# The first mixer of the second block in even and odd tokens, its Fourier half and long convolution as one stage; gates projected in strips, softmax weights blended on queries

## The chip, the cores and the metric

One core of a Trainium2 chip runs the whole program in one launch. TensorE multiplies, VectorE, ScalarE and GpSimd work elementwise, SyncE issues the DMAs. The metric is the device time of one execution in microseconds (us), lower is better. Before the change it is 3509.33 us, the median of 3 runs (3504.07 to 3513.66).

## The reference, cut to what matters

Two blocks of two layers each, 512 tokens, width 1024, all in float32. The change touches four places. Only they are shown.

```python
# first block, layer 0: the gates of the delta rule, from 32 columns of the projection
g = -jnp.exp(a_log) * jax.nn.softplus(a + dt_bias); beta = jax.nn.sigmoid(b)
q = l2norm(q) * DK ** -0.5; k = l2norm(k)
# first block, layer 1: three head groups of window attention, weighed against each other
alpha = jax.nn.softmax(jnp.stack(lses, axis=2), axis=2)
o = (o * alpha[..., None]).reshape(B, S, DSWA_WIDTH)
# second block, layer 0: the mixer, for x (L = 512) and for the context (L = 256)
u_f = proj[..., :512].reshape(B, L, 4, 128)
y_f = jnp.fft.fft2(u_f, axes=(1, 3), norm='ortho').real.reshape(B, L, 512)
x0, x1, v = jnp.split(_dwconv3(proj[..., 512:], conv_w, conv_b), 3, axis=-1)
spectrum = _hyena_filter_spectrum(L, ...)   # h @ w4, times a decay, two-sided, divided by sum |.|, rfft
y_h = x0 * (irfft(rfft(v * x1, n=2 * L) * spectrum)[:, :L] + v * x1 * bias)
return jnp.concatenate([y_f, y_h], axis=-1) @ w_out
```

## The kernel before

Activations lie with features on the 128 partitions and tokens along the free dimension. The program is a row of stages (`Core.stage`). Within a stage each engine has its own instruction list, written by hand, and the engines wait for each other on semaphores. Between stages all engines meet at a barrier (L155 to L157), so a stage ends with its slowest engine and nothing of the next stage begins earlier. Only weights run ahead: SyncE (`stream_weights`) keeps a ring of 4 chunks of 512 KB filled past the stage's end. A large weight product splits both operands into a high and a low part in fp32r and adds three products (L264 to L266). The small transforms are plain F32 products, and each of them leaves two records in the trace.

The stages that the change touches:

- **gdn_gates** (L751). TensorE projects 512 tokens onto 32 gate columns (L778: 4 token chunks times 8 k-tiles, tokens stationary, 32 columns moving). VectorE copies the result (L812) and computes the gates from it, with ScalarE between. GpSimd squares the keys (L803) and ScalarE the queries. TensorE sums the squares in four 32-column strips of the array (L786), VectorE takes reciprocals (L836), TensorE spreads them (L798) and VectorE scales (L846).
- **blend** (L1917). Maxima and sums, queries on partitions, are transposed to 6 rows of heads by 3 x 512 (L1940, L1958). VectorE and ScalarE work the softmax out on 6 partitions (L1961 to L1970). TensorE spreads it over the 9 tiles (L1948), VectorE multiplies (L1974).
- **filter** (L2092). For each of 6 token blocks and 2 directions TensorE makes the taps (L2137), VectorE applies the decay (L2171), ScalarE takes absolute values (L2197), TensorE sums them over partitions with a matrix of ones (L2130). Then come the transforms of the taps (L2151), 40 products of 512 columns, which VectorE scales into `Hr`, `Hi` (L2183). The final norm of the first block rides along on VectorE (L394, L340, L407, L409).
- **mixer_in** (L2223), the input product, is not touched.
- **fourier** (L2286). For each of 4 channel groups TensorE makes 6 half sums (L2310), VectorE copies them (L2331), TensorE mixes tokens (L2320: 8 products of 512 columns for x, 4 of 256 for the context), ScalarE copies out (L2338).
- **hyena** (L2341). VectorE gates (L2404), TensorE transposes to tokens (L2367), transforms (L2379: 32 and 8 products of 512 columns), VectorE multiplies spectra (L2409 to L2412), TensorE transforms back (L2390: 32 of 512 columns, 16 of 256), VectorE adds and gates (L2421, L2424). The tables are loaded by SyncE at the start of each stage (L2213).

## Time and profile before

| | |
|---|---|
| median of 3 runs | 3509.33 us |
| profiled execution | 3512.14 us |
| its span, first to last instruction | 3510.1 us |
| TensorE busy | 3232.0 us (92%) |
| VectorE busy | 1640.7 us (47%) |
| GpSimd busy | 1089.9 us (31%) |
| ScalarE busy | 1019.8 us (29%) |
| mean granted TensorE clock | 0.95 |

The clock is a share of 2.4 GHz; 0.50 is 1.2 GHz, and a stretch in between holds both levels. Busy time of TensorE counts a pipelined product until its end, so neighbours overlap: products are priced here by the distance of their starts. Lines are those of the kernel before. In the trace `ctx` stands for the filter's sines too, which share its memory.

### The profile page before, as it was taken

The numbers are of one execution on the slowest core, as the hardware profiler recorded it, in microseconds if no ns is written. First come the engines' busy times: TensorE is split into PE (matmuls) and PEld (weight loads), VectorE is DVE, ScalarE is ACT, GpSimd is POOL, SyncE is SP. The second block draws the span as 40 slices with busy tenths as digits, with TensorE's granted clock in tenths as the row PEclk, the third lists the DMA queues.
The fourth block names the chain that finished last, engine by engine and source line by source line (L and its number), as shares of the span: only waits on it lengthen the run. The fifth ranks groups of instructions, "written<-read, shape, count | busy, mean of one in ns | idle before, by whom it ended". The sixth has DMA issues, their size and how long they took to land. (4 is left out here: it accounts for less than half of the span.)

```text
span 3510.1 us, 55525 instructions
## 1 busy us (share of the span) xinstructions
PE 3232.0 (92%) x21706; PEld 2523.5 (72%) x21706; DVE 1640.7 (47%) x2413; ACT 1019.8 (29%) x1532; POOL 1089.9 (31%) x518
## 2 busy tenths in 40 slices
PE   7987888999999789999898799999999889899999
PEld 6855666787878567878386368888888433389987
DVE  6834543421131635311675346555555556557741
ACT  4322332212221622122120013222224324343322
POOL 3422112454444024444021012222222015534433
PEclk9978989999999989999899999999999979999999
DMA  3225334222223012222211111111121111122222
GB/s 133 93 91 172 112 126 154 90 96 90 96 88 118 1 63 94 91 91 100 88 60 61 60 36 60 60 66 60 54 66 54 42 46 44 29 79 90 94 85 84
DMA packets 79885, 282.19 MB, mean 80 GB/s; under 512 B 9386, under 2 KB 12272, under 8 KB 78845
## 3 DMA queue, kind: packets, MB, share of 16 engines
q1 hardware_dynamic: 79164, 279.52, 24.2%
q8 instruction: 106, 1.74, 0.2%
q10 hardware_dynamic: 576, 0.62, 0.1%
q14 instruction: 39, 0.31, 0.0%
HBM read 270.12 MB, written 2.12 MB: 78 GB/s over the span
## 5 line engine op out<-in xcount | busy, mean ns | idle before, releaser
L207 POOL TENSOR_TENSOR weights_low<-weight_ring,weights_high 128x1024 fp32r<-128x1024 f32 x359 | 890.7, 2481 | 1825.4 <-ACT weights_high L201 1825.4
L201 ACT ACTIVATE weights_high<-weight_ring 128x1024 fp32r<-128x1024 f32 x372 | 392.2, 1054 | 852.6 <-PE bank L266 842.3
L264 PE MATMUL bank<-ffn_in_high,weights_low 128*128 128x258 f32 (+2 forms) x1408 | 438.3, 311 | 10.6 <-DVE ffn_in_low L470 6.5
L266 PE MATMUL bank<-ffn_in_high,weights_high 128*128 128x258 f32 (+2 forms) x1408 | 437.8, 311 | 0.0
L265 PE MATMUL bank<-ffn_in_low,weights_high 128*128 128x258 f32 (+2 forms) x1408 | 437.4, 311 | 0.0
L264 PEld LDWEIGHTS bank<-ffn_in_high,weights_low 128*128 128x128 f32 x1408 | 266.7, 189 | 26.8 <-issue 7.1
L265 PEld LDWEIGHTS bank<-ffn_in_low,weights_high 128*128 128x128 f32 x1408 | 267.3, 190 | 14.7
L266 PEld LDWEIGHTS bank<-ffn_in_high,weights_high 128*128 128x128 f32 x1408 | 266.1, 189 | 14.2
L264 PE MATMUL bank<-mlp_down_high,weights_low 128*128 128x512 f32 x512 | 200.5, 392 | 8.0 <-DVE mlp_down_low L570 8.0
L264 PE MATMUL bank<-mlp_in_high,weights_low 128*128 128x512 f32 x512 | 201.8, 394 | 6.2 <-DVE mlp_in_low L470 6.2
L264 PE MATMUL bank<-ffn_down_high,weights_low 128*128 128x512 f32 (+1 forms) x528 | 189.6, 359 | 11.9 <-DVE ffn_down_low L570 11.9
L265 PE MATMUL bank<-mlp_in_low,weights_high 128*128 128x512 f32 x512 | 200.5, 392 | 0.0
L266 PE MATMUL bank<-mlp_in_high,weights_high 128*128 128x512 f32 x512 | 200.5, 392 | 0.0
L265 PE MATMUL bank<-mlp_down_low,weights_high 128*128 128x512 f32 x512 | 200.4, 391 | 0.0
L266 PE MATMUL bank<-mlp_down_high,weights_high 128*128 128x512 f32 x512 | 200.3, 391 | 0.0
L570 DVE TENSOR_TENSOR ffn_down_low<-ffn_hidden,ffn_down_high 128x1024 fp32r<-128x1024 f32 (+1 forms) x66 | 101.6, 1569 | 190.4 <-ACT ffn_down_high L527 190.4
L265 PE MATMUL bank<-ffn_down_low,weights_high 128*128 128x512 f32 (+1 forms) x528 | 189.6, 359 | 0.0
L266 PE MATMUL bank<-ffn_down_high,weights_high 128*128 128x512 f32 (+1 forms) x528 | 188.4, 357 | 0.0
L570 DVE TENSOR_TENSOR mlp_down_low<-mlp_hidden,mlp_down_high 128x512 fp32r<-128x512 f32 x64 | 44.2, 693 | 293.4 <-ACT mlp_down_high L527 293.4
L638 DVE SCALAR_TENSOR_TENSOR mlp_relu<-bank,rstd 128x512 f32<-128x512 f32 x64 | 44.2, 690 | 195.9 <-PE bank L266 195.7
L264 PE MATMUL bank<-gdn_in_high,weights_low 128*128 128x512 f32 x256 | 102.4, 400 | 20.0 <-DVE gdn_in_low L470 20.0
L264 PEld LDWEIGHTS bank<-ffn_down_high,weights_low 128*128 128x128 f32 x528 | 101.2, 192 | 27.3 <-issue 12.3
(541 smaller groups left out, 6463.9 us busy)
## 6 DMA issues: line engine op xcount, KB each, us to landing
weight_ring<-in_mod SPq DMA_DIRECT2D x96, 512.0 KB, 4.4
weight_ring<-in_ffn_up SPq DMA_DIRECT2D x88, 512.0 KB, 3.5
weight_ring<-in_mlp_up SPq DMA_DIRECT2D x64, 512.0 KB, 3.5
weight_ring<-in_mlp_down SPq DMA_DIRECT2D x64, 512.0 KB, 3.5
weight_ring<-in_ffn_down SPq DMA_DIRECT2D x44, 512.0 KB, 3.5
weight_ring<-in_gdn_in SPq DMA_DIRECT2D x32, 512.0 KB, 3.5
weight_ring<-in_dswa_in SPq DMA_DIRECT2D x27, 512.0 KB, 3.5
weight_ring<-in_fh_in SPq DMA_DIRECT2D x16, 512.0 KB, 3.5
```

The costliest lines, as they stand in the source:

```text
L201: act.activation(self.high[:, (g.s0 + at) % SPLIT, 0:g.floats], raw, ACT.Copy).then_inc(self.high_ready, 1)
L207: pool.tensor_tensor(self.low[:, slot, 0:g.floats], self.ring[:, (g.c0 + at) % RING, 0:g.floats], self.high[:, slot, 0:g.floats], ALU.subt ...
L264: pe.matmul(bank, wl, ah, start=start, stop=False)
L265: pe.matmul(bank, wh, al, start=False, stop=False)
L266: return pe.matmul(bank, wh, ah, start=False, stop=stop)
L570: last = dve.tensor_tensor(low[:, at % 2, :, lo:lo + tokens], src((n - p * PER_PASS) * KC, KC), high[:, at % 2, :, lo:lo + tokens], ALU.su ...
L638: dve.scalar_tensor_tensor(out=relu[:, at % 2, :], in0=core.ps[at % RING][:, :], scalar=0.0, in1=core.rstd[:, 0, :], op0=ALU.max, op1=ALU. ...
```

## The change

In the mixer all tables over tokens are laid out with the even tokens first and then the odd ones, and only half of the frequencies are computed as products. The sums over the even and over the odd tokens are kept apart. One frequency of the lower half is odd sum plus even sum, its mirror is the difference. This holds for the filter's taps, for the gated input, for the way back, and for the tokens of the Fourier half. `fourier` and `hyena` become one stage, `mixer_middle`, whose TensorE list interleaves them. The inverse tables are loaded into the memory of the forward ones once the forward transforms are done. Divisions by the filter's absolute sums move from the spectra to the results (`inv_sum`), and the sums are made with the taps stationary and two columns of ones moving. In the gates eight products with 32 stationary columns run in four strips of the array, and four products with stacked identities add the strips. In the blend the softmax is done with queries on partitions, and the weights are turned once, split in fp32r, and spread from 18 rows.

```diff
     @block.tensor
     def _(pe):
+        for k in range(KD):
+            m = pe.matmul(strip(core.ps[0], k % 4)[:, :], wab[:, k, :], core.h[:, k, :], start=k < 4, stop=k >= KD - 4)
+        m.then_inc(strip_sums, 1)
+        pe.wait_ge(strips_kept, 1)
         for c in range(NCH):
-            for k in range(KD):
-                m = pe.matmul(ps_ab[:, c, :], core.h[:, k, c * CH:(c + 1) * CH], wab[:, k, :],
-                              start=k == 0, stop=k == KD - 1)
+            m = pe.matmul(ps_ab[:, c, :], by_strip[:, c * CH:(c + 1) * CH], eye, start=True, stop=True)
         m.then_inc(projected, 1)
...
+        dve.wait_ge(strip_sums, 1)
+        dve.tensor_copy(by_strip[:, :], core.ps[0][:, :]).then_inc(strips_kept, 1)
         dve.wait_ge(projected, 1)
         o(dve.tensor_copy(ab[:, :, :], ps_ab))
...
+    @block.gpsimd
+    def _(pool):
+        pool.wait_ge(loaded, 16)
+        pool.tensor_copy(sel[:, :, :], rows[:, :, :]).then_inc(sel_ready, 1)
...
+        act.wait_ge(turned, 1)
+        act.activation(by_residue(high[:, :]), TURNED[0:3 * HG, :].rearrange("h (r m) -> h r m", r=4), ACT.Copy).then_inc(alpha_high, 1)
...
+        near = stats[:, :, 0, :].rearrange("p x (h b) -> p b x h", b=4)
+        for r in range(4):
+            for b in range(4):
+                last = pe.matmul(NEAR[32 * b:32 * b + 32, 2 * HG * r:2 * HG * (r + 1)], core.ident[:, r::4], near[:, b, :, :],
+                                 start=True, stop=True)
+        last.then_inc(reordered, 1)
+        pe.wait_ge(weighed, 1)
+        alphas = maxes.rearrange("p g (h r) -> p r (g h)", r=4)
+        for r in range(4):
+            last = pe.transpose(TURNED[0:3 * HG, r * P:(r + 1) * P], alphas[:, r, :], core.ident[:, :])
+        last.then_inc(turned, 1)
+        pe.wait_ge(sel_ready, 1)
+        pe.wait_ge(alpha_high, 1)
         for n in range(DW_TILES):
             if n >= 4:
                 pe.wait_ge(blended, n - 3)
-            pe.matmul(core.ps[n % 4][:, :], sel[:, n % GT, :], rows[:, n // GT, :], start=True, stop=True).then_inc(spread, 1)
...
+        dve.wait_ge(reordered, 1)
+        o(dve.tensor_copy(stats[:, :, 0, :].rearrange("p x (h r) -> p x h r", r=4),
+                          NEAR[:, 0:8 * HG].rearrange("p (r x h) -> p x h r", r=4, x=2)))
+        o(dve.tensor_reduce(top[:, :], by_group(maxes), AX, ALU.min))
+        dve.tensor_tensor(maxes, over(top), maxes, ALU.subtract).then_inc(centred, 1)
         dve.wait_ge(exped, 1)
...
+        o(dve.tensor_tensor(sums, sums, maxes, ALU.mult))
+        o(dve.tensor_reduce(total[:, :], by_group(sums), AX, ALU.add))
+        o(dve.reciprocal(total[:, :], total[:, :]))
+        dve.tensor_tensor(maxes, maxes, over(total), ALU.mult).then_inc(weighed, 1)
+        dve.wait_ge(alpha_high, 1)
+        dve.tensor_tensor(by_residue(low[:, :]), TURNED[0:3 * HG, :].rearrange("h (r m) -> h r m", r=4), by_residue(high[:, :]),
+                          ALU.subtract).then_inc(alpha_low, 1)
...
+BANDS = [(s, ft) for s, (lo, L, b0, nb) in enumerate(STREAMS) for ft in range(nb // 2)]
+PARITY_BLOCKS = [(s, q, j) for s, (lo, L, b0, nb) in enumerate(STREAMS) for q in range(2) for j in range(nb // 2)]
+def parity_block(n, lo=0):
+    s, q, j = PARITY_BLOCKS[n]
+    return slice(lo + 2 * P * j + q, lo + 2 * P * (j + 1), 2)
+def half_spectrum(pe, banks, table, part, pair, tokens_of):
+    s, ft = BANDS[pair]
+    lo, L, b0, nb = STREAMS[s]
+    for q in range(2):
+for j in range(nb // 2):
+    b = q * nb // 2 + j
+    last = pe.matmul(banks[q][:, :], table.forward(part, s, b, ft), tokens_of(b0 + b), start=j == 0, stop=j == nb // 2 - 1)
+    return last
+def both_halves(dve, part, lower, mirrored, even, odd):
+    first = dve.tensor_tensor(lower, odd, even, ALU.add)
+    if part == 0:
+return first, dve.tensor_tensor(mirrored, even, odd, ALU.subtract)
+    return first, dve.tensor_tensor(mirrored, odd, even, ALU.subtract)
...
-                pe.matmul(ps[4 + s][:, :], core.ones[:, :], ab[:, d, :], start=b == b0 and d == 0,
-                          stop=b == b0 + nb - 1 and d == 1).then_inc(normed, 1)
+                for c in range(G):
+                    col = 2 * (G * s + c)
+                    last = pe.matmul(ps[4][:, col:col + 2], ab[:, d, c * P:(c + 1) * P], core.ones[:, 0:2], start=b + d + c == 0,
+                                     stop=b == BLOCKS - 1 and d == 1 and c == G - 1)
+                last.then_inc(summed, 1)
...
+        for p, (s, ft) in enumerate(BANDS):
+            lo, L, b0, nb = STREAMS[s]
             pe.wait_ge(mixed, b0 + nb)
...
+            for part in range(2):
+                g = 2 * p + part
+                if g == 2:
+                    norm.tensor(pe)
+                    pe.wait_ge(mixed, BLOCKS)
+                if g >= 3:
+                    pe.wait_ge(taken, g - 2)
+                half_spectrum(pe, GROUP(g), dft, part, p, lambda n: f[:, part, n, :]).then_inc(spectra, 1)
...
+        for g in range(2 * len(BANDS)):
+            p, part = g // 2, g % 2
+            H = (Hr, Hi)[part]
+            dve.wait_ge(odd_ready, g + 1)
+            first, second = both_halves(dve, part, H[:, p, 0, :], H[:, p, 1, :], GROUP(g)[0][:, :], odd[:, g % 3, :])
+            second.then_inc(taken, 1)
+            if g == 2:
+                norm.scale(dve, norm_order)
+        dve.wait_ge(summed, 2 * BLOCKS)
+        dve.reciprocal(inv_sum[:, :], ps[4][:, 0:4 * G])
...
+        for g in range(2 * len(BANDS)):
+            act.wait_ge(spectra, g + 1)
+            if g >= 3:
+                act.wait_ge(taken, g - 2)
+            act.activation(odd[:, g % 3, :], GROUP(g)[1][:, :], ACT.Copy).then_inc(odd_ready, 1)
+            if g == 2:
+                norm.roots(act)
...
-def fourier_stage(core, a, tables):
+def mixer_middle_stage(core, a, uh, Hr, Hi, inv_sum, dft, inverse, fourier):
...
+GROUP = lambda g: ((ps[2], ps[3]), (ps[4], ps[5]), (ps[0], ps[1]), (ps[6], ps[7]), (ps[0], ps[1]), (ps[6], ps[7]))[g]
+HALF = lambda m: ps[2 + m % 2][:, 0:2 * P]
+FOURIER = lambda s: ps[4 + s][:, 0:STREAMS[s][1]]
+CONVOLVED = lambda n: ps[2 + n % 2][:, 0:STREAMS[n // G][1]]
...
+        dft.load(sp, dft_loaded)
+        sp.dma_start(chan[:, :], a["fourier_channels"]).then_inc(channels_loaded, 16)
+        fourier.load(sp, fourier_loaded)
+        sp.wait_ge(spectra, 2 * len(BANDS))
+        inverse.load(sp, inverse_loaded)
...
+        def turn(i):
+            n = TURNS[i]
+            s = PARITY_BLOCKS[n][0]
+            pe.wait_ge(gated, i // 2 + 1)
+            if i >= 2:
+                pe.wait_ge(ptok_ready, i - 1)
+            for c in range(G):
+                last = pe.transpose(ps[i % 2][:, c * P:(c + 1) * P], uh[:, 2 * G + c, parity_block(n, START[s])], core.ident[:, :])
+            last.then_inc(turned, 1)
...
+        def halves(gr):
+            for n in range(BLOCKS):
+                m = gr * BLOCKS + n
+                if m >= 2:
+                    pe.wait_ge(halved, m - 1)
+                pe.matmul(HALF(m), tokens(gr, n), chan[:, :], start=True, stop=True).then_inc(half_sums, 1)
+        def mix(gr):
+            pe.wait_ge(halved, (gr + 1) * BLOCKS)
+            for s, (lo, L, b0, nb) in enumerate(STREAMS):
+                if gr:
+                    pe.wait_ge(fourier_kept, 2 * (gr - 1) + s + 1)
+                for q in range(2):
+                    for j in range(nb // 2):
+                        b = q * nb // 2 + j
                         for part in range(2):
...
+                            last = pe.matmul(FOURIER(s)[:, q * L // 2:(q + 1) * L // 2], af[:, gr % 2, b0 + b, part * P:(part + 1) * P],
+                                             fourier.rows(part, s, b), start=j == 0 and part == 0, stop=j == nb // 2 - 1 and part == 1)
+                last.then_inc(fourier_ready, 1)
+        def convolved(n):
+            s, c = n // G, n % G
+            lo, L, b0, nb = STREAMS[s]
+            if n >= 2:
+                pe.wait_ge(y_scaled, n - 1)
+            for q in range(2):
+                for kb in range(nb // 2):
+                    for part, H in enumerate((Hr, Hi)):
+                        last = pe.matmul(CONVOLVED(n)[:, q * L // 2:(q + 1) * L // 2], H[:, b0 // 2 + kb, q, c * P:(c + 1) * P],
+                                         inverse.rows(part, s, kb)[:, q * L // 2:(q + 1) * L // 2],
+                                         start=kb == 0 and part == 0, stop=kb == nb // 2 - 1 and part == 1)
+            last.then_inc(y_sums, 1)
...
+        for i in range(BLOCKS):
+            turn(i)
+        pe.wait_ge(ptok_ready, BLOCKS)
+        pe.wait_ge(dft_loaded, 16 * dft.loads)
+        spectrum(0)
+        spectrum(1)
+        pe.wait_ge(channels_loaded, 16)
+        pe.wait_ge(taken, 1)
+        halves(0)
+        halves(1)
+        pe.wait_ge(fourier_loaded, 16 * fourier.loads)
+        pe.wait_ge(taken, 2)
+        mix(0)
+        spectrum(2)
+        halves(2)
+        mix(1)
+        halves(3)
+        mix(2)
+        mix(3)
+        pe.wait_ge(inverse_loaded, 16 * inverse.loads)
+        pe.wait_ge(products, 2)
+        for n in range(G):
+            convolved(n)
+        pe.wait_ge(products, 3)
+        for n in range(G, 2 * G):
...
+        def odd_sums(g):
+            act.wait_ge(spectra, g + 1)
+            if g >= 2:
+                act.wait_ge(taken, g - 1)
+            act.activation(odd[:, g % 2, :], GROUP(g)[1][:, :], ACT.Copy).then_inc(odd_ready, 1)
...
+        for lo, hi in ((0, T // 2), (T // 2, T), (CTX0, CTX0 + TC)):
+            v = uh[:, 2 * G:3 * G, lo:hi]
+            dve.tensor_tensor(v, v, uh[:, G:2 * G, lo:hi], ALU.mult).then_inc(gated, 1)
+        for p in range(len(BANDS)):
+            if p:
+                dve.wait_ge(products, p)
+            for part in range(2):
+                g = 2 * p + part
+                dve.wait_ge(odd_ready, g + 1)
+                first, second = both_halves(dve, part, X[:, part, 0, :], X[:, part, 1, :], GROUP(g)[0][:, :], odd[:, g % 2, :])
+                second.then_inc(taken, 1)
+            hr, hi = Hr[:, p, :, :], Hi[:, p, :, :]
+            Xr, Xi = X[:, 0, :, :], X[:, 1, :, :]
+            dve.wait_ge(taken, 2 * p + 2)
+            o.add(dve.tensor_tensor(Y[:, :, :], Xr, hr, ALU.mult))
+            o(dve.tensor_tensor(Xr, Xr, hi, ALU.mult))
+            o.add(dve.tensor_tensor(hi, Xi, hi, ALU.mult))
+            o(dve.tensor_tensor(hr, Xi, hr, ALU.mult))
+            o.add(dve.tensor_tensor(Y[:, :, :], Y[:, :, :], hi, ALU.add))
+            o(dve.tensor_tensor(Xr, hr, Xr, ALU.subtract))
+            dve.tensor_tensor(Hr[:, p, 0, :], Y[:, 0, :], Y[:, 1, :], ALU.add)
+            dve.tensor_tensor(Hr[:, p, 1, :], Y[:, 0, :], Y[:, 1, :], ALU.subtract)
+            dve.tensor_tensor(Hi[:, p, 0, :], X[:, 0, 0, :], X[:, 0, 1, :], ALU.subtract)
+            dve.tensor_tensor(Hi[:, p, 1, :], X[:, 0, 0, :], X[:, 0, 1, :], ALU.add).then_inc(products, 1)
...
+parity = np.concatenate([np.arange(0, L, 2), np.arange(1, L, 2)])
+odd, whole_ = odd[parity, :L // 2], whole_[parity, :L // 2]
```

TensorE in the filter stage, before: the last taps (`filt_w`), the absolute sums (`filt_abs`), the transforms (`filt_taps`) and the norm's sum (L349).

```order
L2137 MATMUL bank<-filt_w,ctx 128x512 x2
L2130 MATMUL bank<-filt_abs,ones 128x512 x2
L2137 MATMUL bank<-filt_w,ctx 128x512 x2
L2130 MATMUL bank<-filt_abs,ones 128x512 x4
L2151 MATMUL bank<-filt_taps,filter_dft_x 128x512 x16
L349 MATMUL bank<-mix_h,ones 128x512
L2151 MATMUL bank<-filt_taps,filter_dft_x 128x512 x16
L2151 MATMUL bank<-filt_taps,filter_dft_ctx 128x512 x8
```

The same place now:

```order
L2219 MATMUL bank<-filt_w,ctx 128x512 x2
L2211 MATMUL bank<-ones,filt_abs 128x2 x8
L2219 MATMUL bank<-filt_w,ctx 128x512 x2
L2211 MATMUL bank<-ones,filt_abs 128x2 x16
L2159 MATMUL bank<-filt_taps,filter_dft_x 128x512 x8
L349 MATMUL bank<-mix_h,ones 128x512
L2159 MATMUL bank<-filt_taps,filter_dft_x 128x512 x8
L2159 MATMUL bank<-filt_taps,filter_dft_ctx 128x512 x4
```

The 12 absolute sums of 512 columns are 48 of two columns, and the 40 transforms are 20.

VectorE at the end of the filter stage, now, behind the norm's sums (`rstd`, `x` are the norm's scaling; `filt_odd_sums` the odd sums that ScalarE copied). Before, the products of L407 and L409 had ten scalings of `Hr` and `Hi` around them and a reciprocal of 512 columns (L2179) ahead of each stream.

```order
L2165 TENSOR_TENSOR Hr<-filt_odd_sums,bank 128x512
L2167 TENSOR_TENSOR Hr<-bank,filt_odd_sums 128x512
L407 RECIPROCAL rstd<-rstd 128x512
L409 SCALAR_TENSOR_TENSOR x<-x,params,rstd 128x512 x8
L2165 TENSOR_TENSOR Hi<-filt_odd_sums,bank 128x512
L2168 TENSOR_TENSOR Hi<-filt_odd_sums,bank 128x512
L2165 TENSOR_TENSOR Hr<-filt_odd_sums,bank 128x512
L2167 TENSOR_TENSOR Hr<-bank,filt_odd_sums 128x512
L2165 TENSOR_TENSOR Hi<-filt_odd_sums,bank 128x512
L2168 TENSOR_TENSOR Hi<-filt_odd_sums,bank 128x512
L2264 RECIPROCAL hyena_inv_sum<-bank 128x16
```

Six sums and differences stand behind the norm's scaling.

TensorE between mixer_in and mixer_out, before, from the end of the Fourier stage into the long convolution:

```order
L2320 MATMUL bank<-fourier_dft_x,fourier_half 128x512 x8
L2320 MATMUL bank<-fourier_dft_ctx,fourier_half 128x256 x4
L155 UNCONDITIONAL_BRANCH
L2358 UNCONDITIONAL_BRANCH
L2367 MATMUL bank<-ident,hyena_in 128x128 x24
L2379 MATMUL bank<-gated_tok,dft_x 128x512 x32
L2379 MATMUL bank<-gated_tok,dft_ctx 128x512 x8
```

Now, the beginning of the one stage (`hyena_in` behind L2418 is the memory of the Fourier half sums):

```order
L2392 MATMUL bank<-ident,hyena_in 128x128 x24
L2159 MATMUL bank<-mid_gated_tok,dft_x 128x512 x16
L2407 MATMUL bank<-mid_channels,mix_h 128x256 x4
L2407 MATMUL bank<-mid_channels,mix_h_ctx 128x256 x2
L2407 MATMUL bank<-mid_channels,mix_h 128x256 x4
L2407 MATMUL bank<-mid_channels,mix_h_ctx 128x256 x2
L2418 MATMUL bank<-fourier_dft_x,hyena_in 128x256 x8
L2418 MATMUL bank<-fourier_dft_ctx,hyena_in 128x128 x4
L2159 MATMUL bank<-mid_gated_tok,dft_ctx 128x512 x4
```

The barrier is gone, the transposes and 16 transforms come first, the Fourier half stands between them and the way back, and each mix has half the columns.

## Rows read from the trace of the kernel before

**Rows 1.** By stretches: length; busy of PE, PEld, DVE, ACT, POOL; PEclk; DMA share; GB/s.
```profile
204.90:240.70 35.80, 29.89 (x134) 20.71 (x134) 18.87 (x40) 11.07 (x16) 7.44 (x4) 0.61 0.00 0
1214.40:1251.20 36.80, 20.97 (x42) 8.79 (x42) 22.60 (x23) 1.48 (x1) 0.00 (x0) 0.55 0.00 0
1674.70:1710.50 35.80, 32.15 (x48) 11.08 (x49) 15.66 (x24) 10.42 (x14) 0.00 (x0) 0.68 0.53 193
1710.50:1749.40 38.90, 35.42 (x83) 15.31 (x81) 29.70 (x28) 1.02 (x3) 0.00 (x0) 1.00 0.01 5
...
1898.00:1956.80 58.80, 47.50 (x144) 29.07 (x144) 10.19 (x24) 3.92 (x8) 0.00 (x0) 0.87 0.12 47
1956.80:2053.30 96.50, 78.41 (x200) 38.40 (x200) 35.93 (x53) 3.48 (x6) 0.00 (x0) 0.91 0.14 55
```

**Rows 2.** Timeline, gates stage: start us, us, engine line op out<-in xcount [idle before].
```profile
204.91 12.57 PE L778 MATMUL bank<-w_ab,gdn_h 128*128 128x32 f32 x64 [2.15 <-PEq L157]
217.41 4.88 PE L786 MATMUL bank<-gdn_squares,one_column 128*32 128x512 f32 x32
...
204.89 7.45 POOL L803 TENSOR_TENSOR gdn_squares<-conv 128x1024 f32<-128x1024 f32 x4 [9.77 <-SPq L155]
```

**Rows 3.** Timeline, TensorE: spread of the blend and products of the next stage.
```profile
1234.10 15.70 PE L1948 MATMUL bank<-blend_maxima,head_rows 6*128 6x512 f32 x18 [14.36 <-DVE blend_maxima L1970]
...
1253.43 0.63 PE L265 MATMUL bank<-window_out_low,weights_high 128*128 128x512 f32 x1
1253.85 0.63 PE L266 MATMUL bank<-window_out_high,weights_high 128*128 128x512 f32 x1
```

**Rows 4.** Timeline, filter stage: TensorE, then VectorE, then ScalarE.
```profile
1678.35 7.19 PE L2137 MATMUL bank<-filt_w,ctx 64*128 64x512 f32 x8 [6.82 <-DMA filt_w<-in_filter_w]
...
1702.98 1.98 PE L2130 MATMUL bank<-filt_abs,ones 128*128 128x512 f32 x4
...
1710.53 13.90 PE L2151 MATMUL bank<-filt_taps,filter_dft_x 128*128 128x512 f32 x32
...
1732.80 3.34 DVE L407 RECIPROCAL rstd<-rstd 128x512 f32<-128x512 f32 x1
1736.18 5.39 DVE L409 SCALAR_TENSOR_TENSOR x<-x,params,rstd 128x512 f32<-128x512 f32 x8
...
1709.53 1.28 ACT L353 ACT_TABLE_LOAD   x1
```

**Rows 5.** By stretches, columns as in rows 1, inside the gates and filter stages.
```profile
208.00:211.00 3.00, 3.00 (x16) 3.00 (x15) 0.00 (x0) 2.17 (x3) 3.00 (x3) 0.50 0.00 0
...
1682.00:1690.00 8.00, 8.00 (x10) 2.55 (x9) 3.37 (x5) 1.89 (x3) 0.00 (x0) 0.50 1.06 426
```

**Rows 6.** Timeline, Fourier stage: TensorE, then ScalarE.
```profile
1907.87 3.78 PE L2310 MATMUL bank<-fourier_channels,mix_h 128*128 128x256 f32 x8 [15.91 <-DMA fourier_dft_ctx<-in_fourier_ctx]
...
1915.66 7.03 PE L2320 MATMUL bank<-fourier_dft_x,fourier_half 128*128 128x512 f32 x16
1922.52 1.89 PE L2320 MATMUL bank<-fourier_dft_ctx,fourier_half 128*128 128x256 f32 x8
...
1922.72 0.60 ACT L2338 ACTIVATE mix_h<-bank 128x512 f32<-128x512 f32 x1 [38.15 <-PE bank L2320]
```

**Rows 7.** Timeline, long convolution: TensorE, then VectorE.
```profile
1960.24 4.66 PE L2367 MATMUL bank<-ident,hyena_in 128*128 128x128 f32 x24 [4.87 <-DVE hyena_in L2404]
1972.63 30.28 PE L2379 MATMUL bank<-gated_tok,dft_x 128*128 128x512 f32 x64 [7.73 <-DMA inverse_dft_ctx<-in_inverse_ctx]
...
1956.82 3.37 DVE L2404 TENSOR_TENSOR hyena_in<-hyena_in 128x3080 f32<-128x3080 f32 x1 [18.17 <-PEq L157]
```

**Rows 8.** Timeline, last tiles of the mixer's input product: VectorE, then GpSimd.
```profile
1884.76 2.85 DVE L2277 TENSOR_SCALAR hy_padded<-hy_padded,mixer_shift 128x512 f32<-128x512 f32 x2 [0.16 <-DVE hy_padded L485]
...
1893.24 0.75 DVE L2277 TENSOR_SCALAR hy_padded<-hy_padded,mixer_shift 128x512 f32<-128x512 f32 x2 [0.16 <-DVE hy_padded L485]
...
1884.65 2.40 POOL L214 TENSOR_TENSOR weights_low<-weight_ring,weights_high 128x1024 fp32r<-128x1024 f32 x1 [6.09 <-ACT weights_high L201]
```

More of the change, by code:

```diff
@@ L2089, in scalar, with __init__, tiles, load @@
         act.activation(self.sn[:, :], self.u[:, :], ACT.Sin).then_inc(self.sines, 1)
-def hyena_filter_stage(core, a, sn, Hr, Hi, cs, norm, loads):
+class Tables:
+    loads = 2
+    def __init__(self, a, key, tiles, inverse=False):
+        blocks = lambda L: L // P // 2 if inverse else L // P
+        self.tabs = [t[:, :].rearrange("p (c b n) -> p c b n", c=2, b=blocks(L)) for t, L in zip(tiles, (T, TC))]
+        self.src = a[key + "_x"], a[key + "_ctx"]
+    @staticmethod
+    def tiles(core, ctx, name):
+        return core.sb(name + "_x", [P, T // P * T], ctx), core.sb(name + "_ctx", [P, TC // P * TC], ctx)
+    def load(self, eng, sem):
+        for dst, src in zip(self.tabs, self.src):
+            eng.dma_start(dst, src).then_inc(sem, 16)
+    def rows(self, part, s, b):
+        return self.tabs[s][:, part, b, :]
+    def forward(self, part, s, b, ft):
+        return self.rows(part, s, b)[:, ft * P:(ft + 1) * P]
+BANDS = [(s, ft) for s, (lo, L, b0, nb) in enumerate(STREAMS) for ft in range(nb // 2)]
[16 more added lines that the diff above has]
+    return first, dve.tensor_tensor(mirrored, odd, even, ALU.subtract)
+def hyena_filter_stage(core, a, sn, Hr, Hi, inv_sum, dft, norm, loads):
     with ExitStack() as ctx:
@@ L3308, in program @@
[L3308 to L3309 removed]
+                with ExitStack() as inner:
+                    parts = [core.halves("mix_in", T, inner), core.halves("mix_in_ctx", TC + 2, inner)]
+                    norm = LateNorm(core, [(x, core.h, T, mod[0].gain(0, 0), parts[0]), (xc, core.hc, TC, mod[0].gain(0, 1), parts[1])],
+                                    [mod[0].shift(0, s) for s in range(2)])
+                    mixer_in_stage(core, gemm["fh_in"], norm, parts, uh)
```

336 lines of the change are left out of this document (121 added, 215 removed).

## The prediction

> **What bounds the kernel now.** I read the page's engine table first: TensorE is busy 92% of the span and no other engine half of it, so what leaves TensorE's list counts in full, if the stage stays TensorE's. The query by stretches then gives each touched stage its length, because a barrier closes every stage and a saving in one can't be eaten by another [rows 1]: gates 35.8 us, blend 36.8, filter 35.8 + 38.9, Fourier 58.8, long convolution 96.5. Third came the timelines of these stages, for the prices of products and for who ends last [rows 2 to 4, 6, 7]. Fourth, the clock inside stretches [rows 5]. The reader is to see three kinds of stage: the two of the mixer are TensorE's with holes for DMA and handshakes, the blend is a chain of small steps on 6 partitions, and the filter is half at 1.2 GHz.
>
> Prices: an F32 product of 512 columns takes two records of (1922.52 - 1915.66) / 16 = 0.43 us, so 0.86, at 2.4 GHz, and half of it for 256 columns [rows 6]. At 1.2 GHz it is twice that (15.70 / 9 = 1.74 [rows 3]). An fp32r product at 1.2 GHz starts 0.42 behind its neighbour [rows 3]. VectorE takes 5.39 / 8 = 0.67 per 512 [rows 4] and 3.37 x 1024 / 3080 = 1.12 per 1024 [rows 7], ScalarE 0.60 [rows 6]. A hop between engines I take as 0.2 (TensorE's last product of L2320 for x ends at 1922.7, the copy begins at 1922.72 [rows 6], other hops are longer).
>
> **Middle stage, before 58.8 + 96.5 = 155.3 us.** TensorE's list now: 24 transposes at 4.66 / 24 [rows 7] = 5.2 with ScalarE's copies; 20 transforms x 0.86 = 17.2, with some 2.6 for the low level at their start, as 32 of them took 30.28 for 27.5 [rows 7]; 24 half sums; 4 mixes of 8 x 0.43 + 4 x 0.25 = 4.4, so 17.6; 16 x 2 products of 256 columns and 16 of 128 on the way back, 13.7 + 4.1 = 17.8. The half sums have two banks where they had four and ScalarE in VectorE's place: two products of 0.43, each waiting for the copy two before it (0.38 and two hops), give 0.55 each, 13.2.
> The start: VectorE's first gate is a third of 3.37, TensorE begins at 1.4 and its transforms at 7.4. The tables for them are half of what the Fourier stage loaded, which were there 10 us after that stage began (first product at 1907.87 [rows 6], stage from 1898.0 [rows 1]); with some 2 us of latency in both I expect them at 6, hidden. End of TensorE: 7.4 + 17.2 + 2.6 + 13.2 + 17.6 + 17.8 + 0.6 of hops = 76.4. Then ScalarE, VectorE twice on 256 columns and the barrier, 2.6: **79**. Nothing else is late: VectorE needs 4 x 0.65 + 6 x 1.15 + 4 x 0.65 = 12.1 per band, three bands from 14 to 53, and the first way back at about 58.5 wants two of them. The inverse tables are asked for behind the last transform at 38.5, with 20 us to land. Saving 76.3. Bounds: if the half sums go at 0.43 and the low level costs nothing, 73.5; if every half sum takes a full round of 1.0 and the mixes lose 2 each on waits, 98.
>
> **Filter, before 35.8 + 38.9.** Taps: 12 products unchanged. The sums of absolutes: 48 products x 2 records, each with a 128-column load and two moving columns. The nearest row is L778, which moves 32 columns: 12.57 / 64 = 0.196 per record [rows 2], so 18.9. Before, 12 products of 0.96 (1.98 less the tail, for two) at 2.4 GHz or 1.86 at 1.2 [rows 4]. By level alone this is a draw: the change here is what the level does. While TensorE issued L778 back to back the granted clock was 0.50 [rows 5], and in this stage it stayed at 0.50 from 1682 to 1690 though TensorE was busy all 8.00 us. In that stretch half of the work has only 64 rows; the level rose once blocks with all 128 rows had run, and in the new list there is no such block before the transforms. So I take 1.2 GHz for all of it: taps 12 x 1.78 (7.19 for four [rows 4]) = 21.4, sums 19 to 20.4, handoffs 1, 42 instead of 32.2 from 1678.35 on: +9.8. The Trainium skill, "TensorE: Matmul & The Clock Gate", Part 1, says that sustained TensorE activity brings the full clock; by it the level would rise soon after the stage's start, which is rival B.
> Second half: 8 transforms at the low level's start 9.5, the norm's sum 0.86, 4 more, 13.8. VectorE is then ahead. But the root now stands behind three copies on ScalarE: copy 14.6, its table load 1.28 [rows 4], root, 16.6; reciprocal 3.34 and scaling 5.39 [rows 4] to 25.4; three pairs of sum and difference, 3.8; end and barrier 30.4, VectorE's, against 38.9: -8.5. Filter **+1.3**. Bounds: -13 (level rises as before) to +6 (records of the sums at 0.25, pairs at 2.0).
>
> **Gates, before 35.8.** L778's 12.57 becomes: 8 products in strips, two rounds of four; L786 did four rounds in 4.88 [rows 2], so 2.4; hop, VectorE copy 0.7, hop; 8 records of 0.2, 1.6: 5.1. That is 7.5 earlier, and the VectorE chain behind it moves whole. One cover goes: GpSimd's squares end at 204.89 + 7.45 = 212.3 [rows 2], before the old chain began, but beside the new one (from 210). VectorE beside GpSimd waits: the same two instructions took 2.85 beside a GpSimd piece and 0.75 alone [rows 8]. So 0 to 2.3, I take 1.2. The Trainium skill, "SBUF — State Buffer", section "SBUF: two separate sides", has it as a lock held for the whole GpSimd instruction, which would let VectorE in after the current piece, near the 1.2. Gates **-6.3** (-5.2 to -8.3).
>
> **Blend, before 36.8.** 16 products of 12 columns with 32-column loads: between 1.6 (a quarter of L778's record) and 6.2 (its whole), I take 2.5, as strips overlap [rows 2]. VectorE's seven short steps and ScalarE's exponential on 128 partitions, 72 or 24 wide, 2.9 with hops, in place of four of 1.7 and a reciprocal on 6 partitions; turning 1.0, ScalarE's copy 0.8. The spread: 18 fp32r products x 0.42 = 7.7 instead of 15.70 (1.2 GHz in both [rows 1, 3]); the low half is made beside the first high product, 0.6 shows. Last VectorE step and barrier 1.3; GpSimd casts the selection beside VectorE's steps, 0 to 2.4, taken 1.2: 18. Gain **-18.8** (-15 to -20).
>
> **Sum.** -76.3 + 1.3 - 6.3 - 18.8 = -100.1. The profiled execution took 3512.14 (span 3510.1, 2.0 around it), so 3412.0. It stood 2.8 over the median; half of that off: 3411.
>
> **The rivals.** A is this forecast, its own range 3401 to 3424.
> B: the filter's first half reaches 2.4 GHz as before. For: the old list did, in the middle of it. Against: two-column products move hardly anything, and L778 lost the level with sixteen times as many. First half unchanged instead of +9.8, second part starts at full clock and ends 27 instead of 30.4: 13.2 less, **3398**.
> C: the middle stage becomes a chain of handshakes: half sums at 1.0, a mix waiting for its two copies, way back waiting for VectorE's products. For: ScalarE serves four kinds of bank in a fixed order. Against: every copy is shorter than the products beside it. +15, **3426**.
> D, slower: the low level outlives the stages. If the two-column sums and the short 128-column products put TensorE to 1.2 GHz and it doesn't come back in the GEMMs behind, each us of them costs one more. It decides at about 100 us of such work, i.e. mixer_out and a quarter of the feed-forward product behind it; carried through 150 us the time is 3411 + 150 = **3561**. For: the level fell under a busy TensorE once. Against: the Fourier stage is at full clock within 5 us (0.87 over 58.8 with 10 idle [rows 1]).
> That the sums are not halved is excluded by the order: 20 transforms, halves of columns in all mixes.
>
> **How the numbers follow.** A 0.60, B 0.20, C 0.17, D 0.01, the rest below 3388. The likeliest is 3411. The range goes from 3390, with B and its spread, to 3432, with C. What can be told from no change is 0.3%, 10.5 us. Only D and what lies near it is above 3520: slower 0.01, same 0.01, faster 0.98.
>
> **What would show it.** In the stretches: middle stage 75 to 84 us with TensorE's clock near 0.95 and VectorE under 60% busy; if it is over 90, the waits in front of L2407 or L2418 name C. Filter: the stretch of taps and sums at 0.50 throughout and about 42 us (A) or 32 with 1.00 in its second half (B), then VectorE as the last engine for 10 us with TensorE idle. Gates: L778 in two rounds of 1.2, VectorE steps stretched before 212. Blend: fp32r pairs 0.85 apart. I am wrong in the main point if the middle stage isn't TensorE's, or if products with 8-byte steps between tokens take longer than 0.43 per record of 512 columns, which no row before shows.

## The result, and the profile after

The changed kernel takes **3408.24 us** (median of 4 runs, 3406.26 to 3411.66) against 3509.18 us of the kernel before on the same chip: a ratio of **0.9714**, 95% interval 0.9697 to 0.9731. The forecast was 3411, its range 3390 to 3432. The profiled execution has a span of 3406.2 us at a mean clock of 0.951, against 3510.1 at 0.950: nothing came from the clock as a whole.

The stages by stretches, in the columns of [rows 1]: gates, blend, filter up to its first transform, filter from there, middle stage.

```profile
203.85:234.15 30.30, 23.63 (x94) 10.96 (x94) 20.95 (x41) 11.07 (x16) 7.44 (x5) 0.57 0.00 1
...
1209.15:1225.00 15.85, 10.09 (x54) 6.67 (x54) 9.39 (x17) 1.32 (x2) 1.13 (x1) 0.50 0.02 5
...
1649.40:1695.80 46.40, 42.71 (x120) 27.73 (x120) 17.15 (x25) 9.46 (x13) 0.00 (x0) 0.50 0.35 125
1695.80:1725.20 29.40, 20.27 (x44) 8.75 (x43) 21.76 (x26) 5.55 (x8) 0.00 (x0) 0.85 0.00 0
...
1873.10:1950.40 77.30, 71.14 (x304) 51.87 (x304) 52.58 (x65) 25.47 (x60) 0.00 (x0) 0.95 0.14 53
```

Set against [rows 1], term by term:

| part | before | after | forecast | measured |
|---|---|---|---|---|
| gates | 35.8 | 30.3 | -6.3 | -5.5 |
| blend | 36.8 | 15.85 | -18.8 | -20.95 |
| filter, taps and sums | 35.8 | 46.4 | +9.8 | +10.6 |
| filter, transforms | 38.9 | 29.4 | -8.5 | -9.5 |
| middle stage | 155.3 | 76.65 | -76.3 | -78.65 |
| sum of the four stages | | | -100.1 | -104.0 |

For the middle stage the stretch above begins 0.65 us too early: the first instruction of the stage, the load of a table, starts at 1873.76. From there to the next stage it is 76.65, and these are the marks of [rows 1]; the texts of the runs below still say 77.3. The untouched stages are 0.1 longer (span -103.9). The medians differ by 100.9, since the profiled execution of before stood 2.8 over its median.

TensorE in the middle stage, by start and length, with the pieces in front and the way back left out:

```profile
1875.09 5.72 PE L2392 MATMUL bank<-ident,hyena_in 128*128 128x128 f32 x24 [7.43 <-DVE hyena_in L2513]
...
1881.49 14.00 PE L2159 MATMUL bank<-mid_gated_tok,dft_x 128*128 128x512 f32 x32 [0.69 <-ACT mid_gated_tok L2486]
1895.33 2.26 PE L2407 MATMUL bank<-mid_channels,mix_h 128*128 128x256 f32 x8
...
1902.16 3.62 PE L2418 MATMUL bank<-fourier_dft_x,hyena_in 128*128 128x256 f32 x16
...
1906.50 3.60 PE L2159 MATMUL bank<-mid_gated_tok,dft_ctx 128*128 128x512 f32 x8
1909.93 2.26 PE L2407 MATMUL bank<-mid_channels,mix_h 128*128 128x256 f32 x8
...
1929.67 0.60 PE L2430 MATMUL bank<-dft_x,Hr 128*128 128x256 f32 x2
```

Between the transforms and the way back TensorE has no wait but the handshakes within the half sums, and the other products keep their prices: 16 transforms in 13.84 and 4 in 3.43, a mix in 4.34, the way back in 17.7. TensorE is idle for 5.5 us of 76.65, where the two stages before held 29.4 of idle time in 155.3.

The end of the filter stage, VectorE:

```profile
1711.87 3.35 DVE L407 RECIPROCAL rstd<-rstd 128x512 f32<-128x512 f32 x1 [0.71 <-ACT rstd L353]
1715.26 5.39 DVE L409 SCALAR_TENSOR_TENSOR x<-x,params,rstd 128x512 f32<-128x512 f32 x8
1720.57 0.68 DVE L2165 TENSOR_TENSOR Hi<-filt_odd_sums,bank 128x512 f32<-128x512 f32 x1
...
1724.15 0.26 DVE L2264 RECIPROCAL hyena_inv_sum<-bank 128x16 f32<-128x16 f32 x1
```

TensorE's last four transforms begin at 1712.47 and take 3.60: it is done 8 us before VectorE.

### The profile page after: what moved, and what is told of

Read it like the earlier page. It is cut to its first block and busy times, and to the rows that moved or that the text cites. A ratio compares the mean times of both kernels' runs of the same rounds, so it can differ in the third digit from the quotient of the medians.

```text
span 3406.2 us, 55466 instructions
## 1 busy us (share of the span) xinstructions
PE 3156.1 (93%) x21670; PEld 2507.6 (74%) x21670; DVE 1629.8 (48%) x2395; ACT 1041.5 (31%) x1585; POOL 1089.0 (32%) x519
## 3 DMA queue, kind: packets, MB, share of 16 engines
q1 hardware_dynamic: 79179, 274.35, 24.6%
## 5 line engine op out<-in xcount | busy, mean ns | idle before, releaser
L264 PE MATMUL bank<-ffn_in_high,weights_low 128*128 128x258 f32 (+2 forms) x1408 | 438.4, 311 | 10.6 <-DVE ffn_in_low L470 6.6
L2622 DVE TENSOR_SCALAR ffn_padded<-ffn_padded,ffn_shift 128x512 f32<-128x512 f32 (+1 forms) x88 | 117.4, 1376 | 6.8 <-DVE ffn_padded L485 6.5
```

The source lines that it names most:

```text
L264: pe.matmul(bank, wl, ah, start=start, stop=False)
L2622: o.add(dve.tensor_scalar(dst, dst, shift[:, j % 2, 0, s:s + 1], None, ALU.add))
```

## The experiments

Twelve kernels ran. Each is the changed kernel with the edit shown. A stage length is from the profiled execution, a ratio is against the kernel before on the same chip, with its interval; the changed kernel's is 0.9714 (0.9697 to 0.9731). A ratio tells some 6 us at best: where its interval overlaps the changed kernel's, as with the norm in front, the pairs, the third band and the squares, the reading rests on the stage in the trace alone.

**1. The filter's first stretch: is it the sums, the rows, or neither?** Four kernels; the first stretch goes from the load of the taps' weights to the first transform, the rest from there to the next stage. In the changed kernel and in the five of the twelve that leave this stage alone the taps and sums ran at the prices of 0.50 to the end, so the level there is no accident of one execution.

Absolute sums with 512 moving columns:

```diff
-for c in range(G):
-    pe.matmul(ps[4][:, col:col + 2], ab[:, d, c * P:(c + 1) * P], core.ones[:, 0:2], ...)
+pe.matmul(ps[4 + 2 * s][:, :], core.ones[:, :], ab[:, d, :], ...)
```

> The changed kernel with the absolute sums of the filter stage made as before: 12 products with the ones stationary and 512 columns moving, instead of 48 with two columns moving. ScalarE copies one row of each stream's sum, and 8 products with one row turn them into columns at the end, under VectorE's tail. In the changed kernel the stretch up to the first transform is 46.4 us at a granted clock of 0.50, the rest of the stage 29.4. Theory 1: the two-column products are what keeps the level low, since they move next to nothing. Then the level rises in the middle as in the kernel before: first stretch 33 to 36 with a mean clock of 0.65 to 0.7, the rest 27 to 29, total about 3395. Theory 2: the level in this stage has another cause (the start of the stage, the wait for the first load), and the form of the sums does not matter: first stretch 46 to 48 at 0.50, total 3408 to 3410.

Absolutes added by GpSimd:

```diff
+pool.tensor_tensor(total, total, ab[:, n % 2, :], ALU.add)     # per tap block; TensorE: 8 products at the end
```

> The changed kernel with the absolutes added over the token blocks by GpSimd (12 instructions of 512 columns), so that TensorE has 8 two-column products at the end of the stage in place of 48. Theory 1 (64-row products don't lift the level, by themselves neither): the taps run at 0.50, 12 x 1.78 = 21.4 behind 3.7 of loading; the first transform starts 27 to 28 us after the stage's start instead of 46.4, the rest stays near 29.4; total about 3390. Theory 2 (only the two-column products held the level down, taps of 64 rows and 512 columns lift it): from the middle on 0.9 a product, the first stretch is then VectorE's, 22 to 24, total about 3384. Theory 3: GpSimd's adds hold VectorE up at its products (0.69 each alone): the first stretch is over 31.

Taps with 128 rows:

```diff
+pool.memset(w4[64:128, :], 0.0); pool.memset(sn[64:128, :], 0.0)   # the products then read 128 rows
```

> The changed kernel with the stationary sines and the moving weights of the taps padded with zero rows from 64 to 128, cleared by GpSimd at the stage's start (0.5 to 1.5 us, beside the load). The count of products and of columns stays. Theory 1 (half of the rows is what keeps TensorE at 1.2 GHz): the level rises in the first stretch once a few 128-row products have run, and the first stretch falls from 46.4 to 30 to 38, total 3396 to 3402. Theory 2 (the two-column products keep it low, whatever the rows of the taps): 0.50 throughout, 46 to 48, total 3408 to 3410.

The norm in front:

```diff
+norm.sums(dve)                  # ahead of the first decay product
+norm.tensor(pe); norm.roots(act)    # behind the first taps
+scale_some(b)                   # two tiles behind each block, from the third on
```

> The changed kernel with the final norm of the first block at the beginning of the filter stage: its sums before VectorE's first decay product, the product and the root behind the first taps, the scaling two tiles at a time in VectorE's idle time between the taps. Theory 1 (the end of the stage is VectorE's, with 8.7 us of reciprocal and scaling in it): the stretch behind the first transform goes from 29.4 to 23 to 24, and the first stretch gets 1 to 3 longer by the later first decay product and the product of the norm at 1.2 GHz; total 3404 to 3406. Theory 2 (something else comes last, or the scaling holds up the taps): the first stretch gets 6 or more longer and the total stays at 3408 or above.

| kernel | first stretch, clock | rest, clock | stage | ratio |
|---|---|---|---|---|
| changed | 46.4, 0.50 | 29.4, 0.85 | 75.8 | 0.9714 |
| wide sums | 30.8, 0.79 | 27.6, 0.92 | 58.4 | 0.9664 (0.9648 to 0.9680) |
| GpSimd adds | 26.7, 0.50 | 31.9, 0.87 | 58.6 | 0.9671 (0.9655 to 0.9687) |
| 128 rows | 28.7, 0.80 | 29.7, 0.85 | 58.4 | 0.9672 (0.9656 to 0.9688) |
| norm in front | 48.9, 0.50 | 22.9, 0.87 | 71.8 | 0.9712 (0.9696 to 0.9728) |

TensorE in the kernel with 128 rows, and below it the taps of the kernel in which GpSimd adds:

```profile
1654.11 6.47 PE L2220 MATMUL bank<-filt_w,ctx 128*128 128x512 f32 x8 [6.96 <-DMA filt_w<-in_filter_w]
1660.41 1.84 PE L2212 MATMUL bank<-ones,filt_abs 128*128 128x2 f32 x16
1662.12 1.96 PE L2220 MATMUL bank<-filt_w,ctx 128*128 128x512 f32 x4
```

```profile
1649.05 10.60 PE L2211 MATMUL bank<-filt_w,ctx 64*128 64x512 f32 x12 [6.71 <-DMA filt_w<-in_filter_w]
...
1660.17 7.24 PE L2211 MATMUL bank<-filt_w,ctx 64*128 64x512 f32 x8 [0.52 <-DVE filt_taps L2255]
...
1668.46 3.78 PE L2211 MATMUL bank<-filt_w,ctx 64*128 64x512 f32 x4 [1.05 <-DVE filt_taps L2255]
```

TensorE in the kernel with wide sums:

```profile
1659.71 3.11 PE L2210 MATMUL bank<-filt_abs,ones 128*128 128x512 f32 x4
1662.75 1.98 PE L2217 MATMUL bank<-filt_w,ctx 64*128 64x512 f32 x4
```

With taps of 64 rows and no sums between them TensorE is busy 21.4 of 23.0 us and stays at 0.50 to the last tap, some 0.9 a record. With 128 rows the record falls to 0.45 after 6.3 us, ahead of the first two-column product, and sixteen two-column products take 1.84 where the changed kernel pays 3.57. With 64-row taps and wide sums the level rises too, within 3 us of the first wide sum. So in the kernel with wide sums the first theory holds in its numbers (its first stretch is even shorter), but its reason ("the two-column products are what keeps it low") does not stand alone: without any of them the taps stay low, and with all of them 128-row taps come up. The first theories of the GpSimd and of the 128-row kernel hold, with first stretches somewhat shorter than given. Either edit is worth 17.4 us. What it is in such a list that lets the level rise is left open by these runs. In the GpSimd kernel the rest is 2.5 longer: TensorE has no sums behind the last tap any more, two of VectorE's steps take 0.93 and 1.66 beside the last adds (0.68 alone), and TensorE waits 2.60 for the norm's sums.

With the norm in front the stage gives the first theory's numbers: the rest gets 6.5 shorter, the first stretch 2.5 longer. The 4.0 less in the stage are 0.0011 of the time, less than the total can tell.

**2. The middle stage: what the handshakes and the interleaving are worth.**

```diff
-HALF = lambda m: ps[2 + m % 2][:, 0:2 * P]
+HALF = lambda m: ps[2 + m // 2 % 2][:, m % 2 * 2 * P:(m % 2 + 1) * 2 * P]   # and one copy of 512 for two
```

> The changed kernel with two half sums of a group side by side in one bank, and one copy of 512 columns by ScalarE (0.60 each, as its other copies of that size) in place of two of 256 (0.41 each as they follow each other). In the changed kernel the 24 half sums go at 0.59 each. Theory 1 (the handshake with ScalarE sets that 0.59): they go at 0.43 to 0.46, the middle stage falls from 77.3 to 73.5 to 74.5, the total by 3 to 4. Theory 2 (the products themselves take 0.59, because their stationary tokens are 8 bytes apart): nothing changes, 77.3.

Twelve half sums took (1899.68 - 1894.30) / 12 = 0.45 each instead of (1902.16 - 1895.33) / 12 = 0.57, ratio 0.9709 (0.9692 to 0.9725). The stage is 74.1, from its first table load to the next stage's first copy; the changed kernel is 76.65 by these marks. The handshake set the price, not the 8-byte steps between tokens. The gain in the stage is 2.5 and not 3 to 4, as all 24 had averaged 0.56 and not 0.59; the total can't tell it.

```diff
+HALF = lambda m: ps[2][:, 0:2 * P]
```

> The changed kernel with a single bank for all half sums, so that each waits for the copy of the one before it. It measures the full round which the third case of the prediction priced at 1.0. Theory 1: product 0.43, copy 0.38 and two hops of 0.1 to 0.2 give 1.0 to 1.2 a half sum, the middle stage becomes 77.3 + 24 x (1.0 to 1.2 - 0.59) = 87 to 92, and everything of it shows in the total. Theory 2 (TensorE's list has slack behind the half sums): the stage grows by less than half of that.

The stage takes 99.8, 23.1 more and well over what either theory gave; ratio 0.9775 (0.9754 to 0.9796). TensorE in its first half sums, and two stretches of them in the columns of [rows 1]:

```profile
1898.43 0.71 PE L2407 MATMUL bank<-mid_channels,mix_h_ctx 128*128 128x256 f32 x2 [0.47 <-ACT hyena_in L2476]
1899.61 1.20 PE L2407 MATMUL bank<-mid_channels,mix_h_ctx 128*128 128x256 f32 x2 [0.47 <-ACT hyena_in L2476]
1901.29 1.22 PE L2407 MATMUL bank<-mid_channels,mix_h 128*128 128x256 f32 x2 [0.47 <-ACT hyena_in L2476]
```

```profile
1893.70:1899.60 5.90, 3.49 (x11) 1.44 (x9) 5.80 (x9) 2.41 (x6) 0.00 (x0) 1.00 0.00 0
1901.20:1910.70 9.50, 7.04 (x12) 3.33 (x13) 9.36 (x11) 1.95 (x6) 0.00 (x0) 0.50 0.00 0
```

A round is 1.18 at full clock, within the expectation. Behind five of them the granted clock falls to 0.50, a round becomes 1.69, and the mixes behind start low as well (4.89 for 3.62). The rounds at full clock alone would be 24 x (1.18 - 0.56) = 15 us; the rest of the 23.1 is the level.

```diff
 spectrum(1)
+spectrum(2)
 halves(0); halves(1); mix(0)
-spectrum(2)
```

> The changed kernel with the transforms of the third band directly behind those of the second, and the whole Fourier half behind them. Their banks are free only when VectorE has taken the second band's, which in the changed kernel it does 6 us after TensorE has finished them (1901.6 and 1895.3). Theory 1 (the Fourier half between the bands covers VectorE's products of the first band): TensorE sits idle for about 6 us, and the middle stage goes from 77.3 to 83 to 84. Theory 2 (the interleaving covers nothing, the way back would wait for VectorE or a table anyway, and what is lost in front is won behind): 77 to 78.

```profile
1901.99 5.24 PE L2159 MATMUL bank<-mid_gated_tok,dft_ctx 128*128 128x512 f32 x8 [6.17 <-DVE mid_spectrum L2167]
```

The wait is 6.17, as forecast, and the four transforms behind it take 5.24 instead of 3.60, for the level fell in the gap. Stage 84.6 by the same marks, 8.0 more, and the ratio, 0.9728 (0.9708 to 0.9749), allows that much. The Fourier half between the bands covers VectorE's products.

**3. The gates: who holds the end?**

```diff
-for t in range(H1, TILES, 2): pool.tensor_tensor(sq...)       # four squares, four with ScalarE
+for t in range(12, TILES, 2): pool.tensor_tensor(sq...)       # two squares, six with ScalarE
```

> The changed kernel with two of GpSimd's four squares in the gates stage given to ScalarE (0.97 each, until 211.1 on the time scale of the changed kernel's trace), so that GpSimd is done before VectorE begins its steps on the gates. In the changed kernel the first of these steps takes 1.55 beside GpSimd; the stage is 30.3 us. Theory 1 (that wait of VectorE is on the path that sets the end): the step goes to 0.2 to 0.3 and the stage to 29.0 to 29.4. Theory 2 (the reciprocal of the norm is held equally by the other path, TensorE's 6.4 us of sums of squares at 1.2 GHz and ScalarE's root behind them, which are ready at 216.5 as VectorE is): VectorE's step is short again and the stage stays at 30.0 to 30.4.

The stage takes 29.1, ratio 0.9716 (0.9699 to 0.9734): the first theory, and the total can't tell 1.2. VectorE's four steps are short again and done at 209.0, but ScalarE's exponential behind them begins only at 211.01, right behind its sixth square, so ScalarE now holds the chain. The other executions settle it. In the eight profiled kernels with four squares on GpSimd the strips took from 1.92 to 3.53, by where the clock fell, and the stage 30.2 to 30.3 in all of them. The strips' place was L778 with 12.57 in [rows 2]. Here are VectorE's steps in the kernel with the norm in front, where the strips took 1.92, and GpSimd's squares:

```profile
203.94 7.45 POOL L806 TENSOR_TENSOR gdn_squares<-conv 128x1024 f32<-128x1024 f32 x4 [9.77 <-SPq L155]
...
208.13 1.46 DVE L818 TENSOR_SCALAR gates_u<-ab 128x64 f32<-128x64 f32 x1
...
209.51 1.96 DVE L819 TENSOR_TENSOR gates_u<-ab,params 128x64 f32<-128x64 f32 x1
...
211.50 0.23 DVE L820 TENSOR_SCALAR gates_abs<-gates_u 128x128 f32<-128x128 f32 x1
```

A square takes 1.89, so they end near 205.8, 207.7, 209.5 and 211.4. Two steps of 0.2 end at 209.59 and 211.47: VectorE gets one instruction through per square, and is free when GpSimd has finished. What TensorE gained in front was given back here.

**4. Do the parts add up, and what do they make together?**

```diff
+gdn_gates_stage, blend_stage, head_rows = those of the kernel before
```

> The changed kernel with the gates and the blend as they were before, to see whether the parts add up. Theory 1 (a barrier around each stage keeps them apart): gates 35.8, blend 36.8, the other stages as in the changed kernel, total 26 to 27 above the changed kernel, 3434 to 3436 on the scale of its 3408. Theory 2 (the level of TensorE's clock is carried from the shortened stages into the ones behind them): the total is off from that by 3 or more.

Gates 37.4, blend 36.7, filter 75.8; middle stage as it was; ratio 0.9784 (0.9764 to 0.9803), that is 0.0070 x 3509 = 24.6 us over the changed kernel. The stages alone give 7.1 + 20.8 = 27.9. The gates are 1.6 longer than in [rows 1], as the level came back later in this execution and TensorE's sums of squares took 6.47 instead of 4.88. Nothing shows in the stages behind; the interval of the total, some 7 us wide on each side, holds both expectations. The 3.3 us between stages and total lie between the gates and the blend, where no edit reaches: that piece took 971.1 here and 975.0 in the changed kernel, and from 969.7 to 977.5 over all profiled kernels. The stages between the blend and the filter took 424.6 and 424.4. So the parts add up as far as such scatter lets one see, and whether the gates hand their level on to the next stage stays open.

Last, what the runs pointed to: 128 rows or wide sums or both, the norm's sums in front and its scaling at once behind the last tap, pairs of half sums, five squares with ScalarE.

> The changed kernel with what the runs pointed to. Gates: five of the eight squares with ScalarE and three with GpSimd. Filter: taps padded to 128 rows, absolute sums with 512 moving columns, the norm's sums ahead of VectorE's first decay product, its product and root behind the first taps, its scaling at once behind the last tap, while TensorE makes the first transforms. Middle stage: two half sums in one bank and one copy. Theory 1 (each gain stands by itself): gates 28.4 to 28.9 instead of 30.3, filter 28 to 31 up to the first transform and 23.5 to 25.5 behind it instead of 46.4 and 29.4, middle 74.2 instead of 77.3; total 3379 to 3384 against 3408. Theory 2 (with the first stretch short, VectorE is its bound, and the norm's sums in front only move the wait): first stretch 33 or more, total above 3386.

> The same version, but with the absolutes added by GpSimd in place of the sums with 512 moving columns, so that TensorE has only the padded taps in the first stretch. Theory 1 (TensorE's sums are still on the path): first stretch 24 to 27, the rest 25 to 27, total 3377 to 3382. Theory 2 (VectorE is the bound there and waits beside GpSimd's adds): first stretch 29 or more, no better than the other version.

> The version with sums of 512 moving columns, but with the taps left at 64 rows. It tells what the padding adds once the sums are wide. Theory 1 (with wide sums the level still rises only behind the second block's sums, some 5 us later): first stretch 31 to 33, the rest as in the padded version, total 3382 to 3387, 2 to 3 above it. Theory 2 (the first stretch is VectorE's anyway): no difference between the two.

| kernel | first stretch | rest | stage | total | ratio |
|---|---|---|---|---|---|
| both | 26.7 | 20.5 | 47.3 | 3373.28 | 0.9620 (0.9604 to 0.9637) |
| GpSimd adds, 128 rows | 22.2 | 29.1 | 51.3 | 3377.05 | 0.9635 (0.9615 to 0.9654) |
| wide sums, 64 rows | 33.8 | 20.5 | 54.3 | 3381.46 | 0.9638 (0.9619 to 0.9657) |

The first beats both kernels: 131 us under the one before (3504.38 on its chip). Its stages gain 1.4 (gates 28.9), 28.5 (filter) and 3.3 (middle 73.4) over the changed kernel, 33.2 in all, and the ratio says 0.0094 x 3509 = 33: here the parts add up. Its filter stage, in the columns of [rows 1]:

```profile
1644.96:1671.70 26.74, 23.52 (x51) 9.86 (x52) 22.01 (x28) 11.40 (x15) 1.62 (x2) 0.88 0.59 208
1671.70:1692.22 20.52, 19.38 (x57) 9.18 (x55) 16.75 (x23) 4.65 (x9) 0.00 (x0) 1.00 0.03 11
```

The rest is TensorE's again, 19.38 busy of 20.52, and goes at full clock from its first product, as no stretch of two-column products stands ahead of it. Its 16 transforms of x take 14.08 where they took 16.49 in the kernel with the norm in front, 2.4 of the 3 by which the rest is shorter than expected. The padding is worth 7.0 beside wide sums, more than either theory of the third kernel gave: the level rises 3.5 us behind the first tap with it and 12.9 without, where the norm's product, now ahead of the sums, still runs low (2.07 for 1.13). With GpSimd's adds the first stretch is the shortest, but VectorE's sums and differences come late behind it, and TensorE waits 5.76 for them, so that the rest is longer than expected (25 to 27). Set beside the first kernel with GpSimd's adds it also shows the rows most plainly: TensorE had issued nothing in the stage but four records of padded taps when the level rose, within 3.3 us of the first (0.54 in 1648.9 to 1652.2, 1.00 behind), where the taps of 64 rows stayed at 0.50 for all 24 records. All three intervals lie below that of the changed kernel; among themselves they overlap.

## Why the prediction was right, step by step

- **Middle stage**, forecast 79, measured 76.65. Half sums 13.2 forecast, (1902.16 - 1895.33) + 3.29 + 3.24 = 13.4 measured; mixes 17.6 and 17.55; way back 17.8 and 17.7; TensorE's end 76.4 and 73.65. The term that was mis-sized is the 2.6 for the low level at the transforms: it was already over there (0.54 in 1873.1 to 1881.4, 1.00 behind), and the transforms began at 7.7 for the 7.4 forecast, behind transposes of 5.72 for 5.2. One sign missed: VectorE was busy 52.58 of 76.65 us, 69% and not under 60%, though TensorE did not have to wait for it between the bands. Case C, the chain of handshakes, did not come: what they cost on the half sums is 2.6 in all (13.4 less 10.8 with pairs).
- **Filter, first stretch**: 42 from the first tap forecast, 42.7 measured, at 0.50 throughout. A two-column record took 0.22, not 0.20. Case B, the level rising as before, did not come. The Trainium skill, "TensorE: Matmul & The Clock Gate", Part 1, has sustained activity bring the full clock. These rows do not agree: TensorE was busy 42.71 of 46.40 us at 0.50, and 21.4 of 23.0 with no two-column product at all. The reason given ahead, that no block with all 128 rows runs before the transforms, is borne out only in part: blocks of 128 rows and two columns do run there, and 64-row taps with wide sums between them come up.
- **Filter, rest**: the odd copy behind the norm's product done at 14.6 forecast and 14.0 measured, scaling at 25.4 and 24.8, end 30.4 and 29.4. VectorE last, as said. Moving the norm shows the cover: 6.5 of it goes.
- **Gates**: -6.3 forecast, -5.5 measured. VectorE's copy came 7.0 earlier for the 7.5, and the step beside GpSimd cost 1.4 for the 1.2. That such a sum came near is in part luck: the step that failed is "7.5 earlier" with a chain that "moves whole". The chain starts when GpSimd is done, whatever TensorE gains: between strips of 3.53 and of 1.92 the stage was the same. The Trainium skill, "SBUF — State Buffer", section "SBUF: two separate sides", has the shared port as a lock held for a whole instruction. The rows agree, with steps of 0.2 that take 1.46 and 1.96. What the forecast missed is that the next square held the next step again, so that a chain of short steps pays once for every square still to come.
- **Blend**: 18 forecast, 15.85 measured, the largest miss in its own size and beyond its bound of -20. The products in strips took 0.69 where 2.5 was taken (its low bound was 1.6), and GpSimd's cast of 1.13 ended at 1212.5, 2.4 before TensorE needed it. Of the 1.2 taken for it 0.5 showed all the same, on VectorE: its last step of the weights took 0.71 beside the cast where a step of the same shape takes 0.23. In the eleven other kernels with this blend it took from 0.56 to 0.74, by where the cast lay, and ended 0.1 behind the cast each time.

```profile
1211.02 0.23 DVE L1988 TENSOR_TENSOR neg_maxima_sums<-neg_maxima_sums 128x72 f32<-128x72 f32 x1 [0.33 <-ACT neg_maxima_sums L1952]
...
1211.38 1.13 POOL L1947 CAST blend_head_rows_r<-blend_head_rows 18x1152 fp32r<-18x1152 f32 x1 [77.90 <-DMA blend_head_rows<-in_head_rows]
...
1211.89 0.71 DVE L1991 TENSOR_TENSOR neg_maxima_sums<-neg_maxima_sums,blend_total 128x72 f32<-128x72 f32 x1
```

The spread went as priced, 0.43 a record beside the 0.42 of [rows 3]:

```profile
1216.50 0.62 PE L1974 MATMUL bank<-blend_alpha_high,blend_head_rows_r 18*128 18x512 f32 x1
...
1216.93 0.62 PE L1977 MATMUL bank<-blend_alpha_low,blend_head_rows_r 18*128 18x512 f32 x1
```

- **Sum**: the parts came out 3.9 lower than forecast, the median 2.8; the forecast had taken another 1.0 off the parts' 3412.0, and the untouched stages are 0.1 longer. The errors partly cancel: gates +0.8, filter -0.2, against blend -2.15 and middle -2.35.

## What to carry to other kernels

Price a list of small products at both levels of the clock, and look what ran before the level rose in the old list: an edit that saves columns can cost its whole gain by keeping the stage at 1.2 GHz, and 64 idle rows may be worth filling with zeros. Beside a row of GpSimd instructions, count VectorE's steps, not their time: here each square let one through. A gap or a handshake on TensorE costs itself and then the level.

## What the runs showed of the hardware that was not expected

- Twelve products (24 records) of 64 rows and 512 columns ran at 0.50 for 23 us though TensorE was busy 21.4 of them; the same products with 64 more rows of zeros were at 1.00 after 6.3 us.
- The price of a product of two columns follows the level, 0.22 a record at 0.50 and 0.11 at 1.00. A row of 32 of them let the level fall: 4.76 where twice 1.84 is 3.7, and the transforms behind began at 0.50.
- Gaps of 0.47 in rounds of 1.18 were enough for the level to fall, in a stage that otherwise ran at 1.00 from its transforms on.
- Beside GpSimd's squares or cast a VectorE step of 0.2 on SBUF operands waited for the end of the running instruction (up to 1.96), but a copy out of a bank did not: 0.29 beside the squares (L817) and 0.29 alone (L812 before).
